# Attention heads in pairs: scores in row halves, values in column halves of the array, features on partitions, probabilities normalised first

## The chip, the cores and the metric

One core of a Trainium2 chip runs the whole program. The metric is the device time in microseconds from one launch to its end; lower is better. The engines named below are TensorE (PE, its weight loads are listed as PEld), VectorE (DVE), ScalarE (ACT), GpSimd (POOL) and the DMA queues (SP's and POOL's among them).

## What is computed

Two transformer blocks run one after the other on 256 tokens of 1,024 features. The first has four branches of width 512 (8 heads of 64 features each): a state-space branch and three attentions. Only this part matters here:

```python
def hybrid_mixer(h, w_in, ...):
    proj = h @ w_in
    (m_z, m_xbc, m_dt, b_qkv, c_qkv, c_f, d_q, d_kv, gate_logits) = jnp.split(proj, SPLIT_POINTS, axis=-1)
    y_a = mamba2_branch(...)                 # state space: y = (C B^T * decay) (x dt), then gated and normed
    y_b = moba_attention(...)                # causal softmax(q k^T/8 + bias) v
    y_c = forgetting_attention(...)          # causal softmax(q k^T/8 + cum_i - cum_j) v
    y_d = sliding_window_attention(...)      # 2 key/value heads for 8 query heads, window 128, a sink per head
    branches = jnp.stack([y_a, y_b, y_c, y_d], axis=2)
    branch_out = jnp.einsum('bsiw,iwd->bsid', branches, w_branch)
    gates = jax.nn.sigmoid(gate_logits.reshape(bsz, s_len, N_BRANCHES, D_MODEL))
    return jnp.sum(gates * branch_out, axis=2) @ w_out
```

Behind it come a feed-forward part, the second block (with four more attention heads, "mla" in the code) and its feed-forward part.

## The kernel before

Every large matrix product is split: a float32 operand becomes a high part (a copy to fp32r by ScalarE, `split_high` or `gate_high`) and a low part (the difference, by VectorE, `split_low` or `gate_low`), and TensorE computes high x high, high x low and low x high (`product3`, L617). Weights arrive through a ring of three 2 MB slots on SP's queue; a slot is filled again when its chunk has been split or used.

The attention stage is the loop at L807 over 32 units, one unit being one head of one branch, in the order forgetting attention (branch 2), state space (0), block attention (1), sliding window (3). All 256 x 256 scores of a head that the causal mask leaves are held as 128 x 128 and 128 x 256. For unit u TensorE does, in this order: `scores(u)` (L722) into bank 4 or 5; `probs_T(u - 1)` (L754), three transposes of the previous head's probabilities into bank 6; `gate_piece(u)` (L783), twelve products of 512 columns of the gate projection, which has nothing to do with attention and is spread over the loop as filling; `values(u - 1)` (L765), three products of transposed probabilities (128 x 128 as weights) with 64 columns of v, into bank 7. A head has 64 features, so a score product uses 64 rows of the array; q and k of even heads lie on partitions 0 to 63, those of odd heads on 64 to 127. In the state-space branch the "scores" are decay differences, and POOL multiplies their exponentials with C B^T (L2788) in place of a softmax.

On VectorE the order for each u (L2194) is `bias_scores(u)` (add bias or mask, row minimum), `gate_low(u + 1)`, `finish_head(u - 1)` (divide the output by the row sum, write it with tokens on partitions). On ScalarE (L1625): `exps(u)`, `take_probs_T(u - 1)` (copy of the transposes to SBUF), `gate_high(u + 1)`, and in every second group of two units `take_gate` (reads a finished gate job out of its bank). Two buffers each hold scores, probabilities, their transposes and the high gate parts. Engines work their queues in order, so an instruction that waits holds up all behind it.

After the loop `branch_T` (L818) transposes the branch outputs to features on partitions, 8 transposes of 128 x 128 for each branch, which ScalarE and VectorE take out in two parts, and `branch_product` (L831) multiplies them with the branch weights. POOL's queue also carries `load_bias`, which brings the bias rows of heads from DRAM into HEAD_BIAS (the tile HT) once older heads have been read.

In the rows, ARENA is one large region that holds q, k, v, probabilities and outputs; HN holds the state-space output; PICK_PARTS and DECAY_PARTS are the operands of the decay products; STAT holds row sums.

## Time and profile before

| | |
|---|---|
| runs, us | 1036.4, 1042.77, 1041.92; median 1041.92 |
| profiled execution, us | 1039.39, its span 1037.6 |
| TensorE busy | 975.4 us, 94% of the span |
| VectorE busy | 591.6 us, 57% |
| ScalarE busy | 465.9 us, 45% |
| POOL busy | 77.3 us, 7% |
| mean granted TensorE clock | 0.970 of full |

### The profile page before, as it was taken

What the parts mean: (1) busy time and instruction counts of PE and PEld (TensorE: products, weight loads), DVE (VectorE), ACT (ScalarE), POOL (GpSimd) and SP (SyncE); (2) the same over time, 40 slices, a digit from 0 to 9 for tenths busy, and PEclk for the clock granted to TensorE, in tenths of its full rate; (3) what the DMA queues carried; (4) which work ended last, traced back from release to release, by engine and by line L of the source; (5) the groups of instructions that cost most, each with busy time, mean ns of one, the idle gap of its engine ahead of it and who ended that gap; (6) DMA issues with size and microseconds to landing.
All of it is one profiled execution on the core that took longest, in us unless ns stands there. A gap on an engine that the chain in (4) does not pass through costs nothing. (4 is left out here: it accounts for less than half of the span.)

```text
span 1037.6 us, 16843 instructions
## 1 busy us (share of the span) xinstructions
PE 975.4 (94%) x7121; PEld 861.7 (83%) x7121; DVE 591.6 (57%) x899; ACT 465.9 (45%) x705; POOL 77.3 (7%) x82
## 2 busy tenths in 40 slices
PE   6899999999988988999999799999979889999998
PEld 5889977887767867999988698788868669999887
DVE  3775444453455655555554766877866555665443
ACT  3554334546544435434443446355243454454332
POOL 1000000110000410000000130002451000000000
PEclk9999999999999998999999979999989899999999
DMA  9965542242226534455544423122200044454431
GB/s 362 191 250 197 207 164 81 82 158 106 102 82 250 189 135 154 163 173 207 189 163 171 178 75 152 66 98 82 83 2 3 1 163 163 171 210 187 171 154 41
DMA packets 14746, 149.86 MB, mean 144 GB/s; under 512 B 1664, under 2 KB 3840, under 8 KB 6096
## 3 DMA queue, kind: packets, MB, share of 16 engines
q1 hardware_dynamic: 12448, 139.65, 36.3%
q0 software_dynamic: 1264, 5.24, 2.7%
q10 hardware_dynamic: 960, 3.90, 1.0%
q8 instruction: 57, 0.93, 0.4%
q14 instruction: 17, 0.14, 0.0%
HBM read 144.59 MB, written 4.19 MB: 143 GB/s over the span
## 5 line engine op out<-in xcount | busy, mean ns | idle before, releaser
L2004 DVE TENSOR_TENSOR W_LOW<-weights,W_HIGH 128x2048 fp32r<-128x2048 f32 (+1 forms) x100 | 229.3, 2293 | 244.2 <-ACT W_HIGH L1472 244.2
L1472 ACT ACTIVATE W_HIGH<-weights 128x2048 fp32r<-128x2048 f32 (+1 forms) x100 | 190.8, 1908 | 295.5 <-PE bank L617 295.5
L617 PE MATMUL bank<-OVER_HT,W_HIGH 128*128 128x256 f32 x608 | 173.0, 285 | 1.9 <-DVE OVER_HN L2016 1.9
L617 PE MATMUL bank<-OVER_HN,W_HIGH 128*128 128x256 f32 x608 | 172.6, 284 | 0.0
L617 PE MATMUL bank<-OVER_HT,W_LOW 128*128 128x256 f32 x608 | 172.5, 284 | 0.0
L617 PEld LDWEIGHTS bank<-OVER_HT,W_HIGH 128*128 128x128 f32 x608 | 116.7, 192 | 2.5 <-issue 2.5
L617 PEld LDWEIGHTS bank<-OVER_HN,W_HIGH 128*128 128x128 f32 x608 | 116.8, 192 | 0.0
L617 PEld LDWEIGHTS bank<-OVER_HT,W_LOW 128*128 128x128 f32 x608 | 116.6, 192 | 0.0
L2138 DVE TENSOR_TENSOR RING_LOW<-weights,GATE_HIGH 128x1024 fp32r<-128x1024 f32 x32 | 39.2, 1225 | 72.5 <-ACT GATE_HIGH L1506 72.5
L617 PE MATMUL bank<-W_HIGH,HID_HIGH 128*128 128x512 f32 x200 | 77.9, 389 | 0.0
L617 PE MATMUL bank<-W_LOW,HID_HIGH 128*128 128x512 f32 x200 | 77.9, 389 | 0.0
L617 PE MATMUL bank<-W_HIGH,HID_LOW 128*128 128x512 f32 x200 | 77.9, 389 | 0.0
L617 PE MATMUL bank<-FIRST_HIGH,W_HIGH 128*128 128x256 f32 x240 | 69.3, 289 | 6.2 <-DVE W_LOW L2004 6.1
L617 PE MATMUL bank<-FIRST_HIGH,W_LOW 128*128 128x256 f32 x240 | 68.7, 286 | 0.0
L617 PE MATMUL bank<-FIRST_LOW,W_HIGH 128*128 128x256 f32 x240 | 68.7, 286 | 0.0
L617 PE MATMUL bank<-GATE_HIGH,FIRST_HIGH 128*128 128x512 f32 x128 | 54.3, 424 | 3.7 <-DVE RING_LOW L2138 3.7
L584 PE MATMUL bank<-HT,weights 128*128 128x256 f32 x240 | 53.9, 380 | 0.0
L617 PEld LDWEIGHTS bank<-FIRST_HIGH,W_HIGH 128*128 128x128 f32 x240 | 46.3, 193 | 8.6 <-DVE W_LOW L2004 7.3
L617 PE MATMUL bank<-GATE_HIGH,FIRST_LOW 128*128 128x512 f32 x128 | 51.3, 401 | 0.0
L617 PE MATMUL bank<-RING_LOW,FIRST_HIGH 128*128 128x512 f32 x128 | 51.3, 401 | 0.0
L584 PEld LDWEIGHTS bank<-HT,weights 128*128 128x128 f32 x240 | 45.0, 190 | 6.7 <-issue 0.9
L1544 ACT ACTIVATE ARENA<-bank 128x256 f32<-128x256 f32 (+3 forms) x51 | 21.3, 434 | 56.2 <-PE bank L1261 24.3
(481 smaller groups left out, 1955.4 us busy)
## 6 DMA issues: line engine op xcount, KB each, us to landing
weights<-weights_dram SPq DMA_DIRECT2D x63, 2048.0 KB, 8.0
bias_rows_dram<-ARENA POOLq DMA_DIRECT2D x1, 3072.0 KB, 39.4
weights<-weights_dram SPq DMA_DIRECT2D x2, 1024.0 KB, 6.0
BIAS<-params_dram ACTq DMA_DIRECT2D x1, 1997.0 KB, 11.8
weights<-weights_dram SPq DMA_DIRECT2D x1, 1664.0 KB, 7.8
weights<-weights_dram SPq DMA_DIRECT2D x1, 1584.0 KB, 6.8
X<-x_dram ACTq DMA_DIRECT2D x2, 512.0 KB, 4.0
HT<-bias_rows_dram POOLq DMA_DIRECT2D x1, 1024.0 KB, 7.2
```

The costliest lines, as they stand in the source:

```text
L584: ins = pe.matmul(o, w[:, k, a:a + n], HT[:, k, :], start=(k == 0), stop=(k == KD - 1))
L617: ins = pe.matmul(o, left[a][k], right[b][k], start=(first and k == 0 and a + b == 0), stop=(last and k == n - 1 and a == 1))
L1472: act.activation(piece_parts(k)[0], piece_source(k), ACT.Copy).then_inc(sem("pieces_high"), 1)
L1544: fill_out(act.activation(dst, o[0:rows, 0:n], ACT.Copy, scale=scale), name)
L2004: dve.tensor_tensor(low, piece_source(k), high.bitcast(F32), ALU.subtract)\
L2138: dve.tensor_tensor(low, src, high.bitcast(F32), ALU.subtract).then_inc(sem("gate_split"), 1)
```

## The change

Units go in pairs p of two heads (`NP` = 16 pairs). Per pair TensorE does `pair_scores(p)`, transposes of head 2p - 2, gate piece 2p, transposes of head 2p - 1, gate piece 2p + 1, `pair_values(p - 1)`.

- Scores: the two heads' products of 64 rows stand directly behind each other, one on rows 0 to 63 into bank 4, one on rows 64 to 127 into bank 5. The sliding-window heads are reordered (0, 5, 1, 4, 2, 7, 3, 6), so that a pair has one head of each key/value head. The decay products of forgetting attention follow for both heads.
- Values of the three attentions: v (128 tokens x 64 features) is now the weights and the transposed probabilities are streamed, 256 and 128 columns; the two heads write partitions 0 to 63 and 64 to 127 of bank 7. The output has features on partitions.
- VectorE divides the probabilities by their row sum (`normalise`) before they are transposed; the output is then only copied (`finish_pair`, one copy for a pair, two for a sliding-window pair, since the two have other places).
- The transposes of branches 1 to 3 fall away; their high and low parts are one instruction each on ScalarE and VectorE. Branch 0 (state space) keeps its transposes, now ahead of the last gate piece. The last pair's values stand between the two halves of branch 0's product.
- The second piece of branch 0's weights gets its own place, two bias loads become four, and the last head's transposes use bank 4.
- The four heads of the second block keep their form.

```diff
-BIAS_LOADS = [(0, 8, 0, 0), (8, 4, 0, 20), (12, 4, 4, 24)]
+BIAS_LOADS = [(0, 8, 0, 0), (8, 2, 0, 20), (12, 2, 2, 20), (10, 2, 4, 24), (14, 2, 6, 24)]
...
-UNITS = [(b, h) for b in (2, 0, 1, 3) for h in range(NH)]
+UNITS = [(b, h) for b, heads in ((2, range(NH)), (0, range(NH)), (1, range(NH)), (3, (0, 5, 1, 4, 2, 7, 3, 6)))
+         for h in heads]
+NP = len(UNITS) // 2
...
-FILLS += [(("y_T", i, b), 4 + 2 * (i % 2) + b) for i in range(4) for b in range(2)]
+FILLS += [(("y_T", 0, b), JOB_AT["gate", 6, b] % 4) for b in range(2)]
...
+                     ("branch", 0, 1): (over("BRANCH_HIGH", "ARENA", 14336, [PIECE]), over("BRANCH_LOW", "HT", 0, [PIECE])),
...
+            def scores(units):
+
+                br = ALL_UNITS[units[0]][0]
                 for (c0, c1, q0) in ((0, P, 0), (P, 384, P)):
                     n = c1 - c0
-                    ins = pe.matmul(o[:, c0:c1], q[:, q0:q0 + P], k[:, 0:n], start=True, stop=(br != 2))
+                    for u in units:
+                        q, k = operands(u)
+                        ins = pe.matmul(BK[4 + u % 2][:, c0:c1], q[:, q0:q0 + P], k[:, 0:n], start=True, stop=(br != 2))
+                        if c0 and br != 2:
+                            ins.then_inc(sem("scores_written"), 1)
                     if br == 2:
                         cum = DECAY_PARTS[:, S:2 * S]
-                        pe.matmul(o[:, c0:c1], cum[:, q0:q0 + P], both_parts(h, n, 1), start=False, stop=False)
-                        ins = pe.matmul(o[:, c0:c1], both_parts(h, P, -1), cum[:, 0:n], start=False, stop=True)
+                        for u in units:
+                            o, h = BK[4 + u % 2], ALL_UNITS[u][1]
+                            pe.matmul(o[:, c0:c1], cum[:, q0:q0 + P], both_parts(h, n, 1), start=False, stop=False)
+                            ins = pe.matmul(o[:, c0:c1], both_parts(h, P, -1), cum[:, 0:n], start=False, stop=True)
+                            if c0:
+                                ins.then_inc(sem("scores_written"), 1)
...
+            def pair_scores(p):
+
+                if p:
+                    pe.wait_ge(sem("scores_read"), 2 * p)
+                if UNITS[2 * p][0]:
+                    scores((2 * p, 2 * p + 1))
+                else:
+                    state_scores(2 * p)
+                    state_scores(2 * p + 1)
...
+                if u < NU:
+                    pe.wait_ge(sem("probs_normed"), attention_units(u + 1))
...
+            def pair_values(p):
+
+                br, units = UNITS[2 * p][0], (2 * p, 2 * p + 1)
+                if br == 0:
+                    pe.wait_ge(sem("mix_by_pool"), state_units(2 * p + 2))
+                else:
+                    pe.wait_ge(sem("probsT_by_act"), attention_units(2 * p + 2))
+                if p:
+                    pe.wait_ge(sem("heads_done"), p)
+                o = BK[7][:, 0:S]
+                if br == 0:
+                    for u in units:
+                        ins = token_values(o[:, (u % 2) * P:(u % 2 + 1) * P], u, XDT, UNITS[u][1] * HD)
+                    ins.then_inc(sem("heads_written"), 1)
+                    return
+                V = {1: BV1, 2: CV1, 3: DV1}[br]
+                for n, (c0, k0, k1) in enumerate(((0, 0, S), (P, S, 384))):
+                    for u in units:
+                        h = UNITS[u][1]
+                        a, pb = HD * (h // 4 if br == 3 else h), HD * (h % 2)
+                        ins = pe.matmul(o[pb:pb + HD, c0:S], V[:, n, a:a + HD], PT_[:, u % 2, k0:k1],
+                                        start=(n == 0), stop=(n == 1))
...
+            for p in range(NP):
+                pair_scores(p)
+                if p:
+                    probs_T(2 * p - 2)
+                gate_piece(2 * p)
+                if p:
+                    probs_T(2 * p - 1)
+                if p == NP - 1:
+                    branch_T()
+                gate_piece(2 * p + 1)
+                if p:
+                    pair_values(p - 1)
+            probs_T(NU - 2)
+            probs_T(NU - 1)
...
+                    if i == 0 and dc == 0:
+                        pair_values(NP - 1)
...
+            for p in range(NP):
+                gate_high(2 * p + 1)
+                if p:
+                    take_probs_T(2 * p - 2)
+                exps(2 * p)
+                if p >= 2:
+                    take_gate(*divmod(p - 2, 2))
+                if p:
+                    take_probs_T(2 * p - 1)
+                exps(2 * p + 1)
...
+                gate_high(2 * p + 2)
+                if p == 14:
+                    act.wait_ge(sem("heads_done"), 12)
...
+                act.wait_ge(sem("heads_done"), {1: 12, 2: 4, 3: 16}[i])
+                act.activation(flat(YT_HIGH[i % 2]), flat(YB[i]), ACT.Copy).then_inc(sem("y_high"), 1)
...
+            def normalise(u):
+
+                br, h = UNITS[u]
                 if br == 0:
-                    dve.tensor_tensor(y, o, y, ALU.add).then_inc(sem("heads_done"), 1)
                     return
+                dve.wait_ge(sem("probs_ready"), u + 1)
                 if br == 3:
                     link(dve.tensor_tensor(RSUM[:, u % 2, :], RSUM[:, u % 2, :], ESINK[:, u % 2, :], ALU.add))
                 link(dve.reciprocal(RREC[:, u % 2, :], RSUM[:, u % 2, :]))
-                dve.tensor_tensor(y, o, bc(RREC[:, u % 2, :].unsqueeze(2), [P, TT, HD]), ALU.mult)\
+                for tt, (c0, c1) in enumerate(((0, P), (P, 384))):
+                    ins = dve.tensor_scalar(PB_[:, u % 2, c0:c1], PB_[:, u % 2, c0:c1], RREC[:, u % 2, tt:tt + 1], None,
+                                            ALU.mult)
+                ins.then_inc(sem("probs_normed"), 1)
...
+            def finish_pair(p):
+
+                dve.wait_ge(sem("heads_written"), p + 1)
+                o = BK[7][:, 0:S]
+                for u in (2 * p, 2 * p + 1):
+                    br, h = UNITS[u]
+                    pb = HD * (h % 2)
+                    if br == 0:
+                        y = YB[0][:, :, h * HD:(h + 1) * HD]
+                        ins = dve.tensor_tensor(y, o[:, (u % 2) * P:(u % 2 + 1) * P].rearrange("p (t w) -> p t w", t=TT), y,
+                                                ALU.add)
+                    elif br == 3:
+                        ins = dve.tensor_copy(YB[br][pb:pb + HD, h // 2, :], o[pb:pb + HD, :])
+                    elif u % 2:
+                        ins = dve.tensor_copy(YB[br][:, h // 2, :], o)
+                ins.then_inc(sem("heads_done"), 1)
...
+            for p in range(NP):
+                for n in {8: (0,), 12: (1, 2), 14: (3, 4)}.get(p, ()):
+                    dve.wait_ge(sem(f"bias_in{n}"), 16)
+                bias_scores(2 * p)
+                bias_scores(2 * p + 1)
+                gate_low(2 * p + 1)
+                if p >= 2:
+                    finish_pair(p - 2)
+                normalise(2 * p)
+                normalise_ssd(p)
+                normalise(2 * p + 1)
+                gate_low(2 * p + 2)
+                if p == 14:
                     split_low(PIECE_AT["branch", 0, 0])
...
+                dve.tensor_tensor(flat(YT_LOW[i % 2]), flat(YB[i]), flat(YT_HIGH[i % 2]).bitcast(F32), ALU.subtract)\
+                    .then_inc(sem("y_split"), 1)
```

Where rows stand in the queues, at the three places that the prediction speaks of. Each row has its line, the operation, out<-in, the shape written, and what it waits for.

**Scores of forgetting attention.** TensorE at the start of the attention stage, before: L747 is q times k, L750 and L751 are the decay products, all of one head.

```order
L747 MATMUL bank4<-ARENA 128x128 [waits job_out0,job_out3,job_out1,job_out2,fill_out6,fill_out7,fill_out4,fill_out5,rows_ready]
L750 MATMUL bank4<-PICK_PARTS0_53,DECAY_PARTS_52 128x128
L751 MATMUL bank4<-DECAY_PARTS_52,PICK_PARTS1_54 128x128
L747 MATMUL bank4<-ARENA 128x256
L750 MATMUL bank4<-PICK_PARTS0_53,DECAY_PARTS_52 128x256
L751 MATMUL bank4<-DECAY_PARTS_52,PICK_PARTS1_54 128x256
```

After: L756 is q times k, L763 and L764 are the decay products, of two heads.

```order
L756 MATMUL bank4<-ARENA 128x128 [waits job_out0,job_out3,job_out1,job_out2,fill_out6,fill_out7,fill_out4,fill_out5,rows_ready]
L756 MATMUL bank5<-ARENA 128x128
L763 MATMUL bank4<-PICK_PARTS0_53,DECAY_PARTS_52 128x128
L764 MATMUL bank4<-DECAY_PARTS_52,PICK_PARTS1_54 128x128
L763 MATMUL bank5<-PICK_PARTS0_53,DECAY_PARTS_52 128x128
L764 MATMUL bank5<-DECAY_PARTS_52,PICK_PARTS1_54 128x128
L756 MATMUL bank4<-ARENA 128x256
L756 MATMUL bank5<-ARENA 128x256
L763 MATMUL bank4<-PICK_PARTS0_53,DECAY_PARTS_52 128x256
L764 MATMUL bank4<-DECAY_PARTS_52,PICK_PARTS1_54 128x256
L763 MATMUL bank5<-PICK_PARTS0_53,DECAY_PARTS_52 128x256
L764 MATMUL bank5<-DECAY_PARTS_52,PICK_PARTS1_54 128x256
```

The products on 64 rows of both heads (banks 4 and 5) are neighbours now, and the array goes to 64 rows and back twice for two heads, not twice for each.

**Values and scores of block attention.** TensorE in the middle of that branch, between two gate pieces, before: L777 to L779 are the values of one head, L747 the scores of the next, L762 the transposes of the one before.

```order
L777 MATMUL bank7<-ARENA 128x64 [waits heads_done,probsT_by_act]
L778 MATMUL bank7<-ARENA 128x64
L779 MATMUL bank7<-ARENA 128x64
L747 MATMUL bank5<-ARENA 128x128 [waits scores_read]
L747 MATMUL bank5<-ARENA 128x256
L762 MATMUL bank6<-CST,ARENA 128x128 [waits probsT_by_act,probs_ready]
L762 MATMUL bank6<-CST,ARENA 128x128 x2
```

After: L834 are the values of a pair, L756 the scores of the next pair, L797 the transposes of one head.

```order
L834 MATMUL bank7<-ARENA 64x256 [waits heads_done,probsT_by_act]
L834 MATMUL bank7<-ARENA 64x256
L834 MATMUL bank7<-ARENA 64x128 x2
L756 MATMUL bank4<-ARENA 128x128 [waits scores_read]
L756 MATMUL bank5<-ARENA 128x128
L756 MATMUL bank4<-ARENA 128x256
L756 MATMUL bank5<-ARENA 128x256
L797 MATMUL bank6<-CST,ARENA 128x128 [waits probsT_by_act,probs_normed]
L797 MATMUL bank6<-CST,ARENA 128x128 x2
```

Values and scores of two heads stand at one place, half as often, and the transposes wait for `probs_normed` (VectorE) instead of `probs_ready` (ScalarE).

**VectorE in block attention.** Before, a pass of one head: L2159 and L2161 are the bias and minimum of its scores, L2138 the low part of the next gate piece, L2174 and L2175 the reciprocal and division of the previous head's output.

```order
L2138 TENSOR_TENSOR RING_LOW0_49<-weights0,GATE_HIGH1_94 128x1024 [waits gate_high]
L2174 RECIPROCAL STAT<-STAT 128x2 [waits heads_written]
L2175 TENSOR_TENSOR ARENA<-bank7,STAT 128x2x64 [waits dve_steps]
L2159 ISA ARENA,STAT<-bank5,HT 128x128 [waits probs_ready,scores_written]
L2159 ISA STAT 128x1
L2161 ISA ARENA,STAT<-bank5,HT 128x256
L2161 ISA STAT 128x1
```

After, the part of a pass behind the two heads' bias rows: L2216 is the low part of the second gate piece, L2271 the copy of the outputs of the pair two passes back, L2251 and L2253 the normalising of both heads, and the last row the low part of the next pass's first gate piece.

```order
L2216 TENSOR_TENSOR RING_LOW1_50<-weights1,GATE_HIGH1_96 128x1024 [waits gate_high]
L2271 COPY ARENA<-bank7 128x256 [waits heads_written]
L2251 RECIPROCAL STAT<-STAT 128x2 [waits probs_ready]
L2253 TENSOR_SCALAR ARENA<-ARENA,STAT 128x128 [waits dve_steps]
L2253 TENSOR_SCALAR ARENA<-ARENA,STAT 128x256
L2251 RECIPROCAL STAT<-STAT 128x2 [waits probs_ready]
L2253 TENSOR_SCALAR ARENA<-ARENA,STAT 128x128 [waits dve_steps]
L2253 TENSOR_SCALAR ARENA<-ARENA,STAT 128x256
L2216 TENSOR_TENSOR RING_LOW2_51<-weights2,GATE_HIGH0_95 128x1024 [waits gate_high]
```

A gate piece's low part stood behind one head's bias and ahead of the previous head's division; now one stands behind two heads' bias and one behind both heads' normalising, and the division is on the probabilities, ahead of the transposes.

## Rows read from the trace of the kernel before

**Rows 1.** TensorE by stretch: us from:to, length, busy, records, granted clock, DMA share, GB/s.

```profile
152.47:195.85 43.38, 43.38 (x224) 1.00 0.14 50
195.85:227.62 31.77, 31.77 (x182) 1.00 0.36 134
227.62:313.39 85.77, 79.94 (x392) 0.96 0.31 111
313.39:320.22 6.83, 3.93 (x32) 1.00 0.85 303
```

**Rows 2.** Timeline, forgetting attention: start, us, engine, line, operation, out<-in, shapes, records [idle before].

```profile
162.65 0.48 PE L747 MATMUL bank<-ARENA 64*128 64x128 f32 x2
163.06 0.32 PE L750 MATMUL bank<-PICK_PARTS,DECAY_PARTS 128*128 128x128 f32 x1
...
163.43 0.70 PE L747 MATMUL bank<-ARENA 64*128 64x256 f32 x2
164.06 0.38 PE L750 MATMUL bank<-PICK_PARTS,DECAY_PARTS 128*128 128x256 f32 x1
...
164.39 0.49 PE L762 MATMUL bank<-CST,ARENA 128*128 128x128 f32 x3
```

**Rows 3.** Timeline, block attention, TensorE.

```profile
232.05 0.92 PE L747 MATMUL bank<-ARENA 64*128 64x128 f32 x4
232.90 0.55 PE L762 MATMUL bank<-CST,ARENA 128*128 128x128 f32 x3
...
236.06 0.33 PE L777 MATMUL bank<-ARENA 128*128 128x64 f32 x2
...
236.77 0.37 PE L747 MATMUL bank<-ARENA 64*128 64x128 f32 x1
```

**Rows 4.** Waits of TensorE, 227 to 316 us: total us, times, longest.

```profile
PE bank L617 <- DVE RING_LOW L2138: 3.7, 3, 1.8
```

**Rows 5.** Timeline, second block: products of 64 rows by 256 columns into two banks.

```profile
729.93 2.86 PE L1088 MATMUL bank<-ARENA 64*128 64x256 f32 x24
```

**Rows 6.** Timeline, second block: products with 64-column weights into partition halves, PEld their loads.

```profile
785.03 0.39 PE L1128 MATMUL bank<-ARENA 128*64 128x128 f32 x4
785.14 0.25 PEld L1128 LDWEIGHTS bank<-ARENA,HN 128*64 128x64 f32 x4
785.25 0.39 PE L1128 MATMUL bank<-ARENA,HN 128*64 128x128 f32 x4
...
785.57 0.44 PE L1132 MATMUL bank<-ARENA 64*64 64x128 f32 x4
```

**Rows 7.** Timeline, end of the attention stage and first branch products, TensorE.

```profile
316.79 1.07 PE L827 MATMUL bank<-CST,HN 128*128 128x128 f32 x8 [0.82 <-issue]
317.69 1.04 PE L827 MATMUL bank<-CST,ARENA 128*128 128x128 f32 x8
320.22 0.47 PE L617 MATMUL bank<-W_HIGH,YT_HIGH 128*128 128x512 f32 x1 [1.50 <-DVE YT_LOW L2213]
...
331.23 1.03 PE L827 MATMUL bank<-CST,ARENA 128*128 128x128 f32 x8
332.02 0.48 PE L617 MATMUL bank<-W_HIGH,YT_HIGH 128*128 128x512 f32 x1
```

**Rows 8.** Groups by line, 227 to 313 us: count, busy us, mean ns, idle before.

```profile
L2138 DVE TENSOR_TENSOR RING_LOW<-weights,GATE_HIGH 128x1024 fp32r<-128x1024 f32 x16 | 19.6, 1225 | 42.6 <-ACT GATE_HIGH L1506 42.6
L1506 ACT ACTIVATE GATE_HIGH<-weights 128x1024 fp32r<-128x1024 f32 x15 | 15.7, 1044 | 0.0
...
L1607 ACT ACTIVATE ARENA<-ARENA,STAT 128x256 f32<-128x256 f32 x16 | 7.9, 494 | 0.0
...
L2161 DVE CUSTOM_DVE_ANT_0 ARENA<-bank,HT,STAT 128x256 f32<-128x256 f32 x8 | 3.8, 480 | 0.0
...
L2159 DVE CUSTOM_DVE_ANT_0 ARENA<-bank,HT,STAT 128x128 f32<-128x128 f32 x8 | 2.7, 343 | 0.2 <-PE bank L747 0.2
...
L2191 DVE TENSOR_SCALAR HN<-HN,STAT 128x512 f32<-128x512 f32 x2 | 0.9, 482 | 0.0
```

235 lines of the change are left out of this document (107 added, 128 removed).

## Prediction

> **What bounds the kernel now.** I read three views, in this order: busy time by stretch, the tensor engine's timeline inside one pass, and the waits. First the stretches [rows 1]. The kernel's last instruction hangs on TensorE, so the question is how TensorE spends the attention stage, 152.47 to 313.39 us. In the first two stretches (forgetting attention, then the state-space heads) it is busy 43.38 of 43.38 and 31.77 of 31.77 us: only less work for it can help there. In the third (block attention, then sliding-window attention, 16 units) it is busy 79.94 of 85.77 us at a clock of 0.96. The short fourth stretch, to the first branch product, is busy 3.93 of 6.83 us.
>
> Next the cost of a pass, read as the distance between starts, since ends are modelled and overlap. Forgetting attention [rows 2]: scores of one head run from 162.65 to 164.39, 1.74 us: q times k for 128 columns 0.41, two decay products 0.37, q times k for 256 columns 0.63, two decay products 0.33. Block attention [rows 3]: scores 232.05 to 232.90, 0.85 us; transposes of the previous head and a gate piece 3.16 us; values 236.06 to 236.77, 0.71 us; a pass is 4.72 us. From the third stretch's start to 313.39 there are 15 such passes and the scores, transposes and gate piece of a sixteenth, less one set of transposes of 0.3: 15 x 4.72 + 4.01 - 0.3 = 74.5 us. The stretch has 85.8, so 11.3 us are lost. A clock of 0.96 between the levels 1.2 and 2.4 GHz means 85.8 x 0.04 x 2 = 6.9 us at the low one, which costs half of that, 3.4 us; the other 7.9 are waits. The largest group of them is a gate piece waiting for its low part from VectorE [rows 4].
>
> **The change, part by part.** (a) Scores in row halves. The two heads of a pair use rows 0 to 63 and 64 to 127 and write different banks. The same form stands later in this kernel: 24 records, 12 products of 64 rows by 256 columns, in 2.86 us, 0.24 us each [rows 5]. What such a product costs alone comes from [rows 2]: 256 columns take 0.63 us and 128 take 0.41, so 128 columns stream in 0.22 us, and the 0.19 us on top are the change between 64 and 128 rows. 0.44 alone against 0.24 means that two halves run side by side. In [rows 3] 384 columns (0.66) and one change make the 0.85 us. A block or sliding-window pair then takes 0.85 us where two heads took 1.70: 0.85 saved. In forgetting attention only q times k is packed; the decay products stay, but the changes of row mode are paid once a pair. Four more decay products are bounded by nothing extra but their own stream (0.21 us for two, as in [rows 6]) and by the 0.37 and 0.33 they take now with a mode change; no mode change stands before them, so 0.25 for two. Pair: 0.41 + 0.37 + 0.25 + 0.63 + 0.33 + 0.25 = 2.24 against 3.48, 1.24 saved (1.04 to 1.32).
>
> (b) Values in column halves. Now three products with 128-column weights and 64 streamed columns, 0.71 us a head, 1.42 a pair. After: 64-column weights, 256 and 128 streamed columns, the two heads beside each other. [Rows 6] has this form: four records, the products of two heads with 128 columns each, start 0.22 us apart (785.03, 785.25). 128 + 256 columns are 0.65 us. Entering column mode I price at 0.20, near the 0.19 above, and leaving at 0.10 (785.25 to 785.57 is 0.32, 0.10 beyond the stream). 0.95 a pair, 0.47 saved (0.3 to 0.6).
> The state-space heads are packed in neither way; their pairs keep their products. Sum of (a) and (b): 4 x (1.24 + 0.47) + 8 x (0.85 + 0.47) = 17.4 us.
>
> (c) Branches 1 to 3 need no transposes: 8 transposes each, 0.79 us (331.23 to 332.02) [rows 7], 2.4 us in all. ScalarE and VectorE take the outputs in one 1,024-element instruction instead of four of 256, under 11 us of products a branch.
>
> (d) Normalising first. A head gets two multiplications of its probabilities, 384 elements together; 512 elements in this form take 0.48 us [rows 8], so 0.45 for both with their fixed part, and 0.2 for the reciprocal, ahead of the transposes; the multiplication of the output falls away and a pair leaves in one copy. This is more VectorE work on the path from scores to values, so I laid the queues of one new pass beside each other, t = 0 at its scores. TensorE: scores to 0.85, transposes, gate piece, transposes, second gate piece from 4.3 to 7.2, values to 8.1. VectorE [rows 8]: two bias passes (0.34 + 0.48 each, started 0.75 apart) from 0.8 to 2.3, low part of the second gate piece to 3.5: 0.8 us before it is needed. ScalarE: exponentials of the first head, then the copy of transposes that TensorE ends at 4.4, exponentials of the second head (0.49 us for 256 columns, about 0.9 with the other 128) to 5.9, the high part of the next pass's gate piece to 6.9 (1.04 us each); its low part on VectorE (1.23) to 8.2, needed at 8.1 + 0.85 + 0.3 = 9.2. Behind it stand the next two bias passes, which wait for scores at 8.9 anyway. The busy time of a sliding-window pass is about 6.0 us on VectorE and 5.5 on ScalarE of 8.1. So neither becomes the bound, and most of the 11.3 us goes too: now a gate piece's low part stands behind scores, bias, exponentials and copy of one head and must be there one short pass later; in the new order every gate piece has a pass of 8 us. I leave 0.8 us of waits near the two weight splits, and 1.6 us where the transposes of branch 0 wait for ScalarE to read out the last-but-one gate pair: gain 11.3 - 2.4 = 8.9 us.
>
> (e) The end of the stage. 313.39 to 320.22 is 6.83 us, with work of 0.71 + 0.3 + 0.71 + 0.85 + 0.79 = 3.4 us; 3.5 us are waits for the last head's copy, for VectorE's output and for the split of branch 0, the last of 1.50 us [rows 7]. In the new order branch 0's transposes stand before the last gate piece, and the last values between the two halves of the first product. Gain 3.5 us; the split (about 3 us on both engines) is covered by 2.86 + 0.95 + 0.6 us of work.
>
> Costed at nothing: the four bias loads instead of two on POOL's queue, each issued at least two passes (16 us) before its heads; and the weight loads: a gate chunk feeds four pieces, 16 us a chunk, and the ring holds three.
>
> Sum: 17.4 + 2.4 + 8.9 + 3.5 = 32.2 us. The profiled execution is 1039.39 us (its span 1037.6), so 1007.2; the median of the runs, 1041.92, lies 2.5 us higher and would give 1009.7. I predict 1008 us.
>
> **A rule against it.** [Rows 6] show a weight load of the column-halved form starting at 785.14, while the products begun at 785.03 still stream, and no time is lost. The Trainium skill (TensorE: Matmul & The Clock Gate, Part 3, The mechanism) says that a weight load overlaps products in flight only if its row group differs. In column halves it never differs, and the loads would be exposed. By the rows the sum is as above; by that rule it would be the first rival.
>
> **Rivals.** Weight loads exposed in the value products: four loads take 0.25 us [rows 6], a pair has eight, 0.5 us x 12 pairs = 6 us: 1014 us. For it speaks only that the row's products have 128 columns and these 256; chance 0.10.
> The waits stay: the slack of 0.8 us at the second gate piece and 1.0 at the next is thin, and stretches at the low clock may come back with the waits, as they stand together now at a clock of 0.96. If all of (d) and (e) stays away: 12.4 us, 1020 us; half of it gives 1014. Chance 0.13.
> The halves do not run side by side: then (a) keeps only the mode changes (about 0.2 to 0.6 a pair) and a value pair costs 1.3 + 0.3 us, more than now: 12 to 15 us stay, 1025 to 1028. [Rows 5, 6] speak against it; 0.03.
> Slower than before: VectorE becomes the bound through the four normalising multiplications of a pair, since each pass has a fixed load on it besides. Its pass is 6.0 us with 0.22 us each. It passes TensorE's 8.1 from 0.75 us each, and eats all 32 us (2.7 us a pair over 12 pairs) from 1.4 us each; at 1.6 us each a pass takes 11.5 us and the kernel 1008 + 12 x 3.4 = 1049 us. The 0.48 us for 512 elements speaks against it: 0.02.
> No change: the gain comes back in one later wait, such as for a weight chunk; 0.03, 1040 us. [Rows 1] have the DMA share at 0.31 in the third stretch.
>
> **Chances and range.** Forecast 0.69, with its own range of 1003 to 1012 (bounds of a and b together 3 us either way, 1.7 us for one stretch at the low clock, 2.5 us between profile and median). Then 0.13, 0.10, 0.03, 0.02, 0.03 as above. 1001 to 1018 leaves out the slower half of the second rival and the last three, and a tail of the forecast below. A measurement of this kernel can tell about 1% (10 us): faster 0.94, within 1% 0.04, slower 0.02.
>
> **What would show it.** Block attention: starts of scores of one pair and the next 8.1 us apart, four score products in about 0.85 us, value products of a pair in 0.85 to 0.95. Forgetting attention: 9.5 us a pair against two times 5.5. State-space heads unchanged at 7.9 a pair. TensorE's idle time in the 85.77 us stretch under 3 us at a clock near 1.0. No transposes between branch products. The prediction is wrong if value pairs take 1.4 us, if gate pieces keep waiting for their low part, or if a wait appears before the first branch product.

## The result: 1010.4 us, the forecast right, one wait larger

| | before | after |
|---|---|---|
| median of 4 runs each, us | 1042.35 (1036.4 to 1042.81) | 1010.37 (1009.32 to 1012.23) |
| ratio, 95% interval | | 0.9708 (0.967 to 0.9746) |
| profiled execution, its span, us | 1039.39, 1037.6 | 1010.02, 1008.2 |

The page of after, busy time by engine and the granted clock in 40 slices:

```profile
PE 950.3 (94%) x7049; PEld 838.4 (83%) x7049; DVE 603.2 (60%) x930; ACT 467.3 (46%) x696; POOL 83.4 (8%) x84
PEclk9999999999999789999999789999979889999999
```

TensorE by stretch, columns as in [rows 1]. The first is forgetting attention, then the state-space passes, then the eight passes to the first branch product, the four branch products, the wait behind them, and what follows it:

```profile
151.75:187.56 35.81, 35.81 (x203) 1.00 0.16 59
187.56:219.16 31.60, 31.60 (x181) 1.00 0.40 139
219.16:287.09 67.93, 66.21 (x381) 1.00 0.39 141
287.09:332.07 44.98, 44.98 (x203) 1.00 0.69 270
332.07:337.78 5.71, 0.00 (x1) 0.82 0.23 60
337.78:346.02 8.24, 7.36 (x25) 0.50 0.57 234
```

The third row answers the last two of [rows 1]: 92.6 us (85.77 + 6.83) with 8.7 idle and a clock of 0.96 in the first of them became 67.9 us with 1.7 idle at the full clock. The last pair's values, 0.8 us, now stand behind it. Inside the passes, forgetting attention (answers [rows 2]; an x8 group is four float32 products of two records each) and block attention ([rows 3]). L834 are a pair's values, L756 its q times k, L763 the first decay product, L797 the transposes:

```profile
168.12 0.87 PE L834 MATMUL bank<-ARENA 128*64 128x256 f32 x8
168.92 0.49 PE L756 MATMUL bank<-ARENA 64*128 64x128 f32 x4
169.35 0.32 PE L763 MATMUL bank<-PICK_PARTS,DECAY_PARTS 128*128 128x128 f32 x1
...
171.14 0.49 PE L797 MATMUL bank<-CST,ARENA 128*128 128x128 f32 x3
...
234.26 0.87 PE L834 MATMUL bank<-ARENA 128*64 128x256 f32 x8
235.06 0.93 PE L756 MATMUL bank<-ARENA 64*128 64x128 f32 x8
235.91 0.55 PE L797 MATMUL bank<-CST,ARENA 128*128 128x128 f32 x3
...
242.27 0.87 PE L834 MATMUL bank<-ARENA 128*64 128x256 f32 x8
```

Between starts: the scores of a forgetting pair 2.22 us (168.92 to 171.14) where two heads took 3.48; of a block pair 0.85 or 0.86 where two took 1.70; a pair's values 0.80 where two heads took 1.42; a block pass 8.01 us (234.26 to 242.27). The waits of TensorE from the stage's start to the mixing projection, which in [rows 4] began with 3.7 us for low parts of gate pieces:

```profile
PE bank L947 <- POOL HN L2916: 5.7, 1, 5.7
PE bank L873 <- ACT ARENA L1688: 1.3, 1, 1.3
PE bank L632 <- DVE OVER_HN L2357: 0.9, 1, 0.9
PE bank L632 <- DVE RING_LOW L2216: 0.5, 1, 0.5
```

The first is the surprise. It stands ahead of the transposes of the mixed branches, behind the last of the twelve adds that GpSimd makes to mix them (L2802 before, L2916 after). Before and after side by side, the kernel before first:

```profile
369.18 1.97 PE L883 MATMUL bank<-CST,HN 128*128 128x128 f32 x16 [3.35 <-POOL HN L2802]
372.02 0.47 PE L617 MATMUL bank<-W_HIGH,OVER_HT 128*128 128x512 f32 x1 [0.88 <-DVE OVER_HN L2243]
374.19 0.39 PE L617 MATMUL bank<-W_HIGH,OVER_HT 128*128 128x512 f32 x1
```

```profile
337.78 3.67 PE L947 MATMUL bank<-CST,HN 128*128 128x128 f32 x16 [5.71 <-POOL HN L2916]
342.33 0.76 PE L632 MATMUL bank<-W_HIGH,OVER_HT 128*128 128x512 f32 x1 [0.88 <-DVE OVER_HN L2357]
346.15 0.40 PE L632 MATMUL bank<-W_HIGH,OVER_HT 128*128 128x512 f32 x1
```

After, the wait is 2.36 us longer. From the transposes to the first product it is 4.55 us instead of 2.84 (1.71 more), and the nine products to the next row shown take 3.82 us instead of 2.17 (1.65 more), because the granted clock is 0.50 there (last stretch above). Together 5.7 us. The wait is there in every run that leaves the adds alone (5.7 us in e1 to e4, e8, e10, e11 and e13). The 1.65 us are not: the same nine products take 3.8 to 4.0 us in the changed kernel, e2, e10, e11 and e13, and 2.2 us in e1, e3, e4 and e8. What the change gains is complete before that wait: from the first scores to the end of the last branch product the time falls by 33.0 us.

### The profile page after: what moved, and what is told of

The parts are those of the page before. It is cut to its first block and busy times, and to the rows that moved or that the text cites. A ratio compares the mean times of both kernels' runs of the same rounds, so it can differ in the third digit from the quotient of the medians.

```text
span 1008.2 us, 16698 instructions
## 1 busy us (share of the span) xinstructions
PE 950.3 (94%) x7049; PEld 838.4 (83%) x7049; DVE 603.2 (60%) x930; ACT 467.3 (46%) x696; POOL 83.4 (8%) x84
## 5 line engine op out<-in xcount | busy, mean ns | idle before, releaser
L2082 DVE TENSOR_TENSOR W_LOW<-weights,W_HIGH 128x2048 fp32r<-128x2048 f32 (+1 forms) x99 | 227.5, 2297 | 238.1 <-ACT W_HIGH L1537 238.0
L2216 DVE TENSOR_TENSOR RING_LOW<-weights,GATE_HIGH 128x1024 fp32r<-128x1024 f32 x32 | 40.7, 1272 | 11.9 <-ACT GATE_HIGH L1571 11.9
```

The source lines that it names most:

```text
L2082: dve.tensor_tensor(low, piece_source(k), high.bitcast(F32), ALU.subtract)\
L2216: dve.tensor_tensor(low, src, high.bitcast(F32), ALU.subtract).then_inc(sem("gate_split"), 1)
```

## Experiments

Each is the changed kernel with one edit, or with several joined where that is said; a "..." in a diff marks lines left out. "Stage" is the distance from the start of the first scores to the start of the last pair's values, 151.75 to 292.75, 141.0 us in the changed kernel. Executions of one kernel differ by several us; the stage is 140.97 to 141.03 us in the four kernels that have it unchanged (after, e2, e5, e7), as long as the clock stays full, so small effects are read from the stage. The kernel before was run again beside each group of experiments, at medians of 1038.1 to 1039.2 us instead of the 1042.35 above, and the changed kernel was not. So the ratios say less of small steps than the medians seem to: the interval of the changed kernel overlaps those of e5, e7, e8, e9 and e12.

| run | median, us (range) | ratio to before, 95% interval | stage, us |
|---|---|---|---|
| changed kernel | 1010.37 (1009.32 to 1012.23) | 0.9708 (0.967 to 0.9746) | 141.0 |
| e1_rows_apart | 1012.69 (1011.9 to 1016.29) | 0.9748 (0.9717 to 0.9778) | 148.1 |
| e2_cols_apart | 1010.32 (1009.46 to 1010.99) | 0.9718 (0.9692 to 0.9743) | 141.0 |
| e3_both_apart | 1015.86 (1015.36 to 1016.23) | 0.9773 (0.9743 to 0.9803) | 146.5 |
| e10_scores_split | 1020.46 (1018.74 to 1025.32) | 0.9818 (0.9787 to 0.9849) | 151.7 |
| e11_values_split | 1019.37 (1017.83 to 1020.77) | 0.9799 (0.9773 to 0.9826) | 150.0 |
| e13_both_split | 1030.36 (1025.95 to 1034.51) | 0.9905 (0.9871 to 0.9938) | 162.0 |
| e4_norm_x3 | 1011.85 (1009.24 to 1012.99) | 0.9729 (0.9701 to 0.9758) | 143.1 |
| e5_split_after_add | 1008.01 (1005.61 to 1009.39) | 0.9701 (0.9676 to 0.9726) | 141.0 |
| e7_two_adds_dve | 1006.67 (1003.04 to 1011.87) | 0.9693 (0.9663 to 0.9722) | 141.0 |
| e8_gate_early | 1010.66 (1009.34 to 1012.8) | 0.9731 (0.9707 to 0.9755) | 140.25 |
| e9_best | 1005.13 (1003.58 to 1007.93) | 0.9682 (0.9654 to 0.9709) | 140.2 |
| e12_best | 1005.26 (1001.86 to 1007.23) | 0.9656 (0.963 to 0.9683) | 140.25 |

**One head after the other.** The products of a pair no longer alternate between the halves. e1 does it to the scores, e2 to the values, e3 to both.

```diff
-                    scores((2 * p, 2 * p + 1))
+                    scores((2 * p,))
+                    scores((2 * p + 1,))
```

```diff
-                for n, (c0, k0, k1) in enumerate(((0, 0, S), (P, S, 384))):
-                    for u in units:
+                for u in units:
+                    for n, (c0, k0, k1) in enumerate(((0, 0, S), (P, S, 384))):
```

> The changed kernel, with the score products of a pair's two heads issued one head after the other instead of in turns. In the changed kernel a block-attention pair takes 0.86 us for its scores (227.04 to 227.90) and a forgetting pair 2.21 us. Theory (row halves work side by side only where neighbours use different halves): with one place per pair left where the halves change, the scores cost up to 0.85 us more for each of 8 pairs and up to 1.24 us more for each of 4, that is up to 11.8 us, and less by what the one change of halves per pair still hides (some 0.25 us in each of 12, 3 us): 1019 to 1022 us. Rival (the gain comes only from the heads being grouped, so that the engine waits less): no change, 1010 to 1011 us.

> The changed kernel, with the value products of a pair issued one head after the other (two of 128 and 256 columns for the first head, then two for the second), instead of in turns between the column halves. In the changed kernel the four take 0.80 us for a pair. Theory (column halves work side by side only if neighbours use different ones): one head's 384 columns took 0.85 us in the scores of the kernel before, so a pair would take about 1.2 to 1.7 us and the 12 pairs 5 to 11 us more: 1015 to 1021 us. Rival (the columns of an array half are free work, whatever the order, since the products are short): no change.

> The changed kernel with both scores and values one head after the other: what the regrouping in pairs, the direct layout of the values and the probabilities normalised first are worth without halves side by side. If the prediction's parts are right (17.4 us for packing, 14.8 us for the rest, of which some 5 us were given back at the transposes of the mixed branches), it stands 9 to 12 us below the kernel before, at 1030 to 1033 us if all overlap goes, 1024 to 1030 if one change of halves per pair still overlaps. If instead VectorE or ScalarE limited the stage behind TensorE, the time would be less than the sum of the two experiments on one part each.

The theory of both runs missed, and so did both figures given for e3 (1015.86 us against 1024 to 1033). In e2 nothing changed, as its rival had it: 0.80 us a pair still. In e1 the timeline shows a block pair unchanged and a forgetting pair back at the old cost of two heads (1.83 us for one, 173.09 to 174.92, where it was 1.74):

```profile
173.09 0.49 PE L756 MATMUL bank<-ARENA 64*128 64x128 f32 x2
173.50 0.32 PE L763 MATMUL bank<-PICK_PARTS,DECAY_PARTS 128*128 128x128 f32 x1
...
174.92 0.49 PE L756 MATMUL bank<-ARENA 64*128 64x128 f32 x2
...
233.95 0.93 PE L756 MATMUL bank<-ARENA 64*128 64x128 f32 x8
234.81 0.55 PE L798 MATMUL bank<-CST,ARENA 128*128 128x128 f32 x3
```

The eight records of the block pair still take 0.86 us, though the first head's two products now stand ahead of the second's in the program. The first record of a product starts at 233.95 us and that of another product of 128 columns 0.01 us behind it, where the program has the first head's 256 columns in between; whether TensorE or something ahead of it brings them together, the records do not tell. In forgetting attention, where decay products over all 128 rows stand behind each score product, a pass is 10.70 us instead of 9.32, 1.38 more; four of them are the 5.5 us by which stage (146.5) and median of e3 are longer. (e1's stage holds 1.6 us more: in that execution the clock was 0.96 from 152 to 196 us. Its median is only 2.3 us above the changed kernel, below the 5.5 of e3. Its profiled execution takes 3.4 us less behind the tenth product of the mixing projection, where the code is the same.) This gave a third theory: TensorE runs two neighbours in different halves at once in whatever order they come, until work on the whole array stands between them.

**Whole-array work between the heads.** e10 puts the transposes of a probability block between the two heads' scores, e11 puts a gate piece between their values, e13 both.

```diff
-                    scores((2 * p, 2 * p + 1))
+                    scores((2 * p,))
+                    if p:
+                        probs_T(2 * p - 2)
+                    scores((2 * p + 1,))
```

```diff
...
+                parted = p and UNITS[2 * p - 2][0]
+                if parted:
+                    pair_values(p - 1, 0)
                 gate_piece(2 * p + 1)
                 if p:
-                    pair_values(p - 1)
+                    pair_values(p - 1, 1 if parted else None)
```

> The changed kernel, with the three transposes of a probability block, which use all 128 rows, put between the score products of a pair's two heads. In the kernel with the scores one head after the other a block-attention pass took 8.02 us as in the changed kernel, and the scores of both heads 0.86 us, while a forgetting pass, where two products over all 128 rows stand behind each of the scores, took 10.70 us and not 9.32. Theory (two neighbours in different halves run together however they are ordered, until an operation on the whole array stands between them): the second head's 0.85 us are paid in the 8 block and sliding passes, 7 of which have a block to transpose in front and one more in the last state-space pass: 6.4 to 6.8 us more, 1016.5 to 1017.5 us. Rival (the regrouping in pairs, not the halves, is what shortened the passes): a block-attention pass stays at 8.0 us, no change.

> The changed kernel, with the value products of a pair's first head ahead of a gate piece (24 products over the whole array) and those of the second head behind it. Both heads' take 0.80 us together now. Theory (they run together, and one head's alone would take those 0.80 us as well): 11 pairs by 0.80 us, 8.8 us more, 1018 to 1019.5 us. Rival (in each half they are short because they are short products, one behind the other): 1010 to 1012 us.

> The changed kernel with both: scores and values of a block or sliding pair apart, with work on the whole array between the heads (forgetting pairs: the values alone). If the two prices are additive, 15 to 16 us above the changed kernel, 1025 to 1026.5 us, and with the 5.5 us of the forgetting scores the halves are worth some 21 us, against the 17.4 us of the prediction. Rival (one cover is used twice, since VectorE or ScalarE comes next): 1019 to 1022 us.

The expectations for e10 and e13 left out that the edit also sets the forgetting heads' scores apart, as e1 does, and that fits how far both medians lie above them (1020.46 against 1016.5 to 1017.5, 1030.36 against 1025 to 1026.5). That of e11 came true (1019.37). e10's timeline, one block pair's scores, and then e11's, one head's values:

```profile
250.46 0.92 PE L756 MATMUL bank<-ARENA 64*128 64x128 f32 x4
251.31 0.55 PE L800 MATMUL bank<-CST,ARENA 128*128 128x128 f32 x3
251.79 0.92 PE L756 MATMUL bank<-ARENA 64*128 64x128 f32 x4
252.64 0.50 PE L632 MATMUL bank<-GATE_HIGH,FIRST_HIGH 128*128 128x512 f32 x1
```

```profile
239.82 0.86 PE L834 MATMUL bank<-ARENA 128*64 128x256 f32 x4
240.62 0.38 PE L756 MATMUL bank<-ARENA 64*128 64x128 f32 x2
```

One head's four records take 0.85 us (scores) or 0.80 (values), what the eight of both heads take in the changed kernel (0.85 and 0.80): the second head costs nothing beside the first. Apart, a block pass is 9.05 us in e10 (+1.04: 0.85, and 0.48 instead of 0.31 for the transposes between) and 8.99 in e11 (+0.98: 0.80, and 0.18 that I put down to a second change into the column form). The stage of e10 is 10.7 us longer: 5.5 for the forgetting heads and 7 x 1.04 (the eighth block pair has nothing to transpose between its heads), less 2.1 that vanish in the longer passes: the 1.3 us at L873 became 0.2, and two passes of 8.27 and 8.75 us in the changed kernel are as long as their neighbours here. That of e11 is 9.0 longer (11 x 0.97, less 1.7 in the same way), that of e13 21.0 (5.5 + 7.3 + 10.7 = 23.5, less 2.5). The prices add up but for those 1.7 to 2.5 us, as the theory has it, and the rivals (grouping alone does it, e10; short products behind one another do it, e11) fall: against e13's order, side by side is worth 21.0 us of the stage. With e13's order the kernel is only 1% faster than before: the direct layout of the values costs more when the heads stand apart (1.77 us a pair against 1.42: one head's 0.80 and the 0.97 by which a pass is longer), which takes back part of the waits and transposes saved.

**Room on VectorE.** e4 multiplies the probabilities three times over.

```diff
+                for _ in range(2):
+                    for c0, c1 in ((0, P), (P, 384)):
+                        ins = dve.tensor_scalar(PB_[:, u % 2, c0:c1], PB_[:, u % 2, c0:c1], 1.0, None, ALU.mult)
+                    link(ins)
```

> The changed kernel with VectorE's multiplications of the probabilities three times over (the two added ones by 1.0, so the result is that of the changed kernel). They took 0.55 us for the two pieces of a head, so 2.2 us of VectorE's time and four more waits for its own result are added to each attention pair, of 8.0 to 9.3 us. The prediction's bound: VectorE has room up to 0.75 us for each multiplication (0.27 now, 0.8 here with its repeats). Theory (the multiplications are hidden, with a little less room than that): 0 to 8 us more, and the waits of TensorE would appear at the gate pieces behind VectorE's weight splits. Rival (VectorE is the limit of the stage already): 12 pairs by 2.2 to 2.6 us, 26 to 31 us more, 1037 us or above.

```profile
PE 953.8 (94%) x7049; PEld 842.4 (83%) x7049; DVE 622.5 (62%) x1026; ACT 467.6 (46%) x696; POOL 83.5 (8%) x84
```

19.3 us of VectorE's time (622.5 less 603.2) cost TensorE 2.1 us of the stage; waits for gate pieces' low parts (1.2 us instead of 0.5) and one more of 0.7 are most of it. So nine tenths of the added work is hidden, and the normalising itself (0.55 us a head) is well inside the room: VectorE isn't the bound.

**The wait at the mixing adds.** In the changed kernel GpSimd's last add (L2916) and VectorE's split of the second weight piece of the projection (L2082) meet (timelines of both engines):

```profile
333.19 4.53 POOL L2916 TENSOR_TENSOR HN<-HN,ARENA 128x512 f32<-128x512 f32 x2
334.11 2.50 DVE L2082 TENSOR_TENSOR W_LOW<-weights,W_HIGH 128x2048 fp32r<-128x2048 f32 x1
```

In the kernel before they met as well, and the other one lost:

```profile
366.63 2.50 POOL L2802 TENSOR_TENSOR HN<-HN,ARENA 128x512 f32<-128x512 f32 x2
367.86 3.41 DVE L2004 TENSOR_TENSOR W_LOW<-weights,W_HIGH 128x2048 fp32r<-128x2048 f32 x1 [0.40 <-ACT W_HIGH L1472]
```

Alone an add takes 1.26 to 1.30 us and the split 2.29. Before, the two adds took 2.50 us and the split 3.41; now the split takes 2.50 and the adds 4.53, of which the last has 3.31.

What turned the order round is in the same traces. The split starts 2.03 us behind the end of the branch products before and 2.04 after. The last add started 0.01 us ahead of it before (367.85) and 0.30 behind it after (334.42). The adds come later because the split ahead of them, on whose engine their operands are made, met an add as well and took 2.60 us. In the kernel before that split began as the adds ended, and took 2.29:

```profile
359.96 2.56 POOL L2802 TENSOR_TENSOR HN<-HN,ARENA 128x512 f32<-128x512 f32 x2 [2.88 <-DVE ARENA L2235]
362.43 2.29 DVE L2004 TENSOR_TENSOR W_LOW<-weights,W_HIGH 128x2048 fp32r<-128x2048 f32 x1 [1.95 <-ACT W_HIGH L1472]
```

```profile
326.58 2.56 POOL L2916 TENSOR_TENSOR HN<-HN,ARENA 128x512 f32<-128x512 f32 x2 [2.83 <-DVE ARENA L2349]
328.69 2.60 DVE L2082 TENSOR_TENSOR W_LOW<-weights,W_HIGH 128x2048 fp32r<-128x2048 f32 x1 [1.58 <-ACT W_HIGH L1537]
```

The split behind the first mixing add met it too (2.68 us): without the transposes between the branch products (0.79 us) VectorE has 0.85 us to spare ahead of that split where it had 1.52. A longer split delays the products and adds behind it, and so the next split meets one again. No run takes this chain apart. e5 keeps the last add and the last split apart, e7 gives the last two adds to VectorE (and takes them out of GpSimd's loop).

```diff
+            dve.wait_ge(sem("mixed_by_pool"), 12)
             split_low(PIECE_AT["out1", 0, 1])
```

```diff
+                    if i == 3 and j >= 2:
+                        wait_job_out(dve, job)
+                        dve.wait_ge(sem("mixed_by_pool"), 5 + j)
+                        dve.tensor_tensor(mix, mix, TMP[:, n % 2, :], ALU.add).then_inc(sem("mixed_by_dve"), 1)
...
```

> The changed kernel, with VectorE's split of the second weight piece of the mixing projection put behind GpSimd's last mixing add (a wait ahead of it). In the changed kernel this split (334.11 to 336.61) and the add (334.42 to 337.7, 3.31 us where the others take 1.27 to 1.30) ran at once, and TensorE waited 5.7 us. Theory (the two slow each other): the add takes 1.3 us again, the wait is 3.6 us, the clock is granted in full for the transposes that follow, and the kernel is 3 to 5 us faster, 1005 to 1007 us. Rival (the add is long for another reason, its own operand being late): no change. Second rival: the split is now late itself and holds up the first products behind the transposes, half of the gain is lost, 1008 us.

> The changed kernel, with the last two of the twelve mixing adds on VectorE itself, each right behind the product that it adds. Two adds of 128x512 on VectorE, some 0.65 us each by its operations of that shape next to them; TensorE's wait ahead of the transposes of the mixed branches should fall from 5.7 us to 2.2 to 2.8 us. Theory: 3 to 3.5 us of wait and the low clock behind it (1.7 us in the transposes, 1.65 us in nine products) are saved, 5 to 6.5 us, 1004 to 1005.5 us. Rival (the clock falls for the shorter wait too): 3 to 3.5 us, 1007 us.

e5's GpSimd and split, and its TensorE by stretch from the end of the branch products on:

```profile
332.06 3.71 POOL L2917 TENSOR_TENSOR HN<-HN,ARENA 128x512 f32<-128x512 f32 x3 [2.83 <-DVE ARENA L2349]
335.81 2.29 DVE L2082 TENSOR_TENSOR W_LOW<-weights,W_HIGH 128x2048 fp32r<-128x2048 f32 x1 [1.69 <-POOL HN L2917]
```

```profile
332.20:335.80 3.60, 0.00 (x0) 0.98 0.06 23
335.80:340.20 4.40, 3.52 (x16) 0.63 0.33 65
340.20:344.00 3.80, 3.78 (x16) 1.00 0.98 418
```

Three adds in 3.71 us, the last no longer than the others, and the wait 3.66 instead of 5.71 us. So it is the meeting that made the add long; its operand was there. The clock still fell for the transposes, against the theory, but was full again for the products. The median is 2.4 us lower, less than the theory's 3 to 5 and at the second rival's 1008, but its mechanism isn't there: the split ends at 338.10 us, and VectorE waits another 1.28 us for the transposes. From the first scores to the tenth product of the mixing projection the profiled execution takes 3.85 us less. In e7 the wait is 3.13 us (theory 2.2 to 2.8), the clock fell all the same, and the median is 3.7 us lower, near the 1007 of its rival (3.60 us less to the tenth product). There the first of VectorE's adds met one of GpSimd's and took 1.26 us, the second 0.69:

```profile
333.36 1.26 DVE L2355 TENSOR_TENSOR HN<-HN,ARENA 128x512 f32<-128x512 f32 x1
334.55 0.68 DVE L2350 SCALAR_TENSOR_TENSOR ARENA<-ARENA,bank 128x512 f32<-128x512 f32 x1
335.26 0.69 DVE L2355 TENSOR_TENSOR HN<-HN,ARENA 128x512 f32<-128x512 f32 x1
```

**The wait for the gate product, and the joined versions.** e8 has ScalarE read that gate product ahead of the exponentials of head 30; e9 joins e7 and e8; e12 has e8's edit, only the last add on VectorE, and the first eight transposes as soon as their half of the adds is done.

```diff
+                if p == NP - 1:
+                    take_gate(6, 1)
                 exps(2 * p)
-                if p >= 2:
+                if 2 <= p < NP - 1:
                     take_gate(*divmod(p - 2, 2))
```

```diff
...
-            pe.wait_ge(sem("mixed_by_pool"), 12)
             for b in range(4):
+                if b == 0:
+                    pe.wait_ge(sem("mixed_by_pool"), 10)
+                if b == 2:
+                    pe.wait_ge(sem("mixed_by_pool"), 11)
+                    pe.wait_ge(sem("mixed_by_dve"), 1)
...
```

> The changed kernel, with ScalarE's reading of the gate product for which TensorE waits 1.27 us in the last pass put ahead of the exponentials of head 30, in a place where ScalarE is idle for 1.83 us. Theory: the wait goes, and 0.9 to 1.3 us with it (the split of the first branch's operand ends 286.04 and would be the next to be late, at about 285.8): 1009.2 us. Rival (another wait takes its place at once): no change.

> The changed kernel with both: the last two mixing adds on VectorE, and the gate product read early. If the two are independent, the sum: 6 to 7.5 us below the changed kernel, 1003 to 1004.5 us. If what is gained in the last pass is waited for again at the mixing adds, no more than with the adds alone.

> The changed kernel with the gate product of the last pass read early, the last mixing add alone on VectorE (in the run with two of them there, the first took 1.26 us beside an add of GpSimd's, and held up the product behind it), and the transposes of the first half of the mixed branches started as soon as the adds of that half are done. Theory: against the kernel with two adds on VectorE (median 1005.13 us, transposes from 334.34 us, the first product of the projection at 337.19 us), the last add is done 0.4 us sooner, and the 1 us of the first eight transposes moves into the wait: 1.2 to 1.5 us less, 1003.7 to 1004 us. Rival (the clock or the split of the weight piece takes the gain back): 1005 us or above.

e8: the 1.27 us at L873 are gone, a wait at a gate piece grew from 0.5 to 0.9 us, and the stage is 0.75 us shorter; the median can't tell it. e9: a median 5.2 us below the changed kernel, less than the forecast 6 to 7.5; its five executions (1003.58 to 1007.93) all lie below those of the changed kernel, though the intervals of the ratios overlap (0.9682 and 0.9708). To the tenth product its profiled execution takes 6.7 us less, which fits the sum. e12 isn't faster than e9:

```profile
332.60 1.09 PE L951 MATMUL bank<-CST,HN 128*128 128x128 f32 x8 [1.22 <-POOL HN L2926]
334.44 1.06 PE L951 MATMUL bank<-CST,HN 128*128 128x128 f32 x8 [0.76 <-POOL HN L2926]
337.29 0.47 PE L632 MATMUL bank<-W_HIGH,OVER_HT 128*128 128x512 f32 x1 [1.79 <-DVE OVER_HN L2367]
```

The waits for the adds fell to 2.0 us, but the first product starts at 337.29 as in e9 (337.19, the stages starting at 151.81 and 151.65): VectorE is still at the split of the weight piece, which ends at 336.55, and the low parts of the transposes (L2367) come behind it. The wait had a second one right behind it; e12's rival holds.

## Why the prediction was right, step by step

- (a) Scores: 1.26 saved a forgetting pair against 1.24, 0.85 a block pair against 0.85. Halves side by side, shown by e1, e10 and e13. Held.
- (b) Values: 0.80 us a pair, 0.62 saved where the sum had 0.47 and its range ended at 0.6. The mechanism was right (e11), the term mis-sized: 128 + 256 columns priced at 0.65 and 0.30 for the two mode changes; the changes cost 0.15 in all. By whole passes (a) and (b) are 4 x (11.1 - 9.32) + 8 x (9.44 - 8.02) = 18.5 us against 17.4.
- The first rival (weight loads exposed) fell. The eight weight loads of a pair's values take 0.13 to 0.14 us each, and eight of them and all products fit in 0.80 us. By the rule of the Trainium skill (TensorE: Matmul & The Clock Gate, Part 3, The mechanism) a load overlaps only products of another row group; here all loads use all rows, in different columns, and they are hidden: the measurement decides against the rule for this form. Nor does the kernel's ordinary form, 128 rows and 128 columns, keep to it: PEld and PE are busy 838.4 and 950.3 of 1008.2 us on the page above, more than the span together, so most loads run beside products.
- (d) and (e): up to the first branch product, with the last pair's values counted, the distance from the first scores fell from 167.75 to 136.14 us, 31.6 us. Less the 18.5 of packing and 0.8 for the set of transposes that stood there, 12.3 us, against 8.9 + 3.5 = 12.4. Held, the left-over wait for ScalarE too (1.3 against 1.6), and the third stretch has the full clock.
- (c): the other two sets of transposes, 1.58 us; the branch products end 1.4 us closer to their start, values not counted. Held, so 33.0 us at the last branch product against 32.2.
- What the sum lacked: the mixing adds. They were on no list, since the change leaves them alone; it moved their phase against VectorE's split, and 5.7 us went back. That is more than the 2.4 us between forecast and median. Against it stand two things that I did not forecast: the stage starts 0.7 us earlier, and behind the ten first products of the projection the kernel is 1.4 us shorter. 33.0 - 5.7 + 0.7 + 1.4 = 29.4, the difference of the spans. Both are no more than executions of the same code differ by. In the changed kernel and its experiments, whose code is the same there, the stage starts between 151.49 and 153.17 us, and the part behind the tenth product takes 658.6 to 666.6 us, around the 663.4 of the kernel before. In one stretch of feed-forward products, twenty steps from one of VectorE's weight splits to the next take 113.92 us before (411.40 to 525.32) and 112.64 after (384.65 to 497.29), but also 113.92 in e2, e3 and e5 and 115.20 in e8. So these 2.1 us are luck. The time fell into the forecast range (1003 to 1012 us) although the sum lacked a term of 5.7 us: the range, 0.8 us more gained in the stage than forecast, and those 2.1 us covered it.
- The last rivals: VectorE as the bound fell with e4. The waits inside the stage went as forecast, so the second rival fell too. "The gain comes back in one later wait" was right in kind, but for 5.7 us and not for all of it, and at an add of GpSimd's, 45 us behind the stage, not at a weight chunk.

## What to carry to other kernels

Two small products in different halves of the array cost here what one of them costs, as long as no work on the whole array comes between; their order among themselves made no difference, so write them in the order that suits semaphores. When a change moves a stage in time, list every place behind it where VectorE and GpSimd both read two operands from SBUF, and see which of the two will come first: the sum of the changed stage doesn't show it. A wait taken away is worth only its distance to the next one on the same engine (e12), so look at that one before the edit. And before explaining a microsecond far from the change, compare runs whose code is the same there.

## What the runs showed of the hardware

- Row halves and column halves need no alternation. Two heads' products, issued as first head, first head, second head, second head, took 0.86 us (rows) and 0.80 us (columns), as when alternated, and as one head alone.
- VectorE and GpSimd hold each other up when both take two operands from SBUF: an add of 1.27 us took 3.31 (changed kernel), a split of 2.29 took 3.41 (before), an add of 0.69 on VectorE took 1.26 (e7). The one that starts first keeps its time, and the other one's is its own plus the rest of the first's, less some 0.15 us: 2.19 + 1.27 against 3.31, 1.26 + 2.29 against 3.41, 0.72 + 0.69 against 1.26. VectorE's product in between, which reads one operand from a PSUM bank, took its 0.68 us beside an add. The Trainium skill (SBUF — State Buffer, SBUF: two separate sides) describes it as an exclusive lock on a shared pair of ports, held for a whole instruction. The trace agrees, with those sums. e5 shows that here an order of the two by a semaphore was cheaper than the race.
- The granted clock after a wait of TensorE: 3.35 us in the kernel before, and full clock; 5.71 us after, and 0.50 for the next 8 us; 3.13 us in e7 and in e9, with and without the fall. The first row is e7, the second e9:

```profile
339.40:344.00 4.60, 4.60 (x11) 0.50 0.85 345
```

```profile
337.20:342.00 4.80, 4.80 (x21) 1.00 0.97 358
```

The length of the wait alone doesn't decide it, nor how long the clock stays down: behind the same 5.71 us the transposes start at 337.78 in the changed kernel and the clock is 0.50 for 8 us more, and in e8 the nine products further on take 2.17 us, as at the full clock. 11 products in 4.6 us against 21 in 4.8 is what it costs while it lasts. The slowest of e7's six executions (1011.9 us) has the lowest mean granted clock, 0.961, and the fastest (1003.0) the highest, 0.973; in which stretches they differ is not shown, since one was profiled.
- The time of TensorE's products at a granted clock of 1.00 isn't the same in every execution: the same twenty steps from weight split to weight split in a stretch of feed-forward products take 112.64 us in the changed kernel, e4, e7 and e10, 113.92 in the kernel before, e2, e3 and e5, and 115.20 in e8. The cause is open.
